# Three expert blocks issued at the release of their own places, in a hybrid mixer and mixture-of-experts layer

## The reference, cut to what matters

```python
logits = (t @ p['router_w'] + p['router_b']).astype(jnp.float32)
top_v, top_i = lax.top_k(logits, TOP_K)              # 4 of 32
for e in range(N_EXPERTS):                           # 32 experts, each 1024x2048 and 1024x1024
    gu = t @ p['moe_w_gu'][e] + p['moe_b_gu'][e]
    glu, lin = jnp.split(gu, 2, axis=-1)
    ...
    y = y + gates[:, e:e + 1] * (act @ p['moe_w_down'][e] + p['moe_b_down'][e])
```

## Time and profile before

| | us |
|---|---|
| median of 3 runs | 1330.65 |
| lowest, highest | 1329.86, 1331.6 |
| the profiled execution, its own time | 1328.54 |
| its span | 1326.6 |
| TensorE matmul busy | 1245.0 (94%) |
| VectorE, ScalarE busy | 400.6 (30%), 263.3 (20%) |

### The profile page before, as it was taken

The page is one execution under the profiler, slowest core; times in us unless marked ns, Lnnn a source line. Parts: engine busy times, 40 slices in busy tenths (PEclk is TensorE's granted clock), DMA queues, the critical chain, the costliest instruction groups (busy, mean ns, idle before and its releaser), DMA issues.

```text
span 1326.6 us, 21403 instructions
## 1 busy us (share of the span) xinstructions
PE 1245.0 (94%) x9094; PEld 588.9 (44%) x9094; DVE 400.6 (30%) x896; ACT 263.3 (20%) x595; POOL 54.2 (4%) x88
## 2 busy tenths in 40 slices
PE   5999999989999999999999999999989999999987
PEld 3456666678885333333333333333333333333333
DVE  1555756755443111122111121211122111122112
ACT  2333208553324110011010011100111010011001
POOL 0031200311200000000000000000000000000000
PEclk9999999999999999999999999999999999999999
DMA  9673420142369999999999999999999999999995
GB/s 385 259 293 147 163 100 0 67 128 69 105 249 373 423 428 426 428 426 427 430 427 427 429 428 427 430 428 427 429 427 427 428 427 427 427 428 428 426 427 237
DMA packets 38378, 453.97 MB, mean 342 GB/s; under 512 B 4288, under 2 KB 4544, under 8 KB 10016
## 3 DMA queue, kind: packets, MB, share of 16 engines
q1 hardware_dynamic: 38304, 452.86, 82.0%
HBM read 451.79 MB, written 1.05 MB: 341 GB/s over the span
## 4 chain that ended last, share of the span: by engine, by line
PE 82%; DMA 8%; DVE 6%; issue 2%; ACT 1%; SPq 0%; DVEq 0%
PE PS L1965 79%; DMA arena<-in_moe_w_gu 5%; DMA arena<-in_moe_b_down 2%; PE PS L2852 1%; DVE arena L1858 1%; DMA arena<-in_ada_first 1%; DVE arena L1861 1%; DVE arena L1864 1%; PE PS L2843 1%; DVE arena L1335 1%; DVE arena L1857 1%; PE PS L2447 0%; DVE arena L1958 0%; PE PS L1977 0%; ACT arena L984 0%
## 5 line engine op out<-in xcount | busy, mean ns | idle before, releaser
L1965 PE MATMUL PS<-arena 128*64 128x512 f32 (+11 forms) x8790 | 1209.2, 415 | 41.1 <-DMA arena<-in_ada_first 15.0
L1965 PEld LDWEIGHTS PS<-arena 64*64 64x64 f32 (+6 forms) x8790 | 559.2, 148 | 642.3 <-issue 576.4
L1857 DVE TENSOR_SCALAR arena<-PS 128x256 f32<-128x256 f32 x64 | 38.7, 604 | 510.5 <-PE PS L1965 510.5
L1167 ACT ACTIVATE arena<-arena 128x256 f32<-128x256 f32 x64 | 26.7, 417 | 482.0 <-DVE arena L1857 482.0
L1886 DVE TENSOR_TENSOR arena<-PS,arena 128x512 f32<-128x512 f32 x32 | 22.2, 692 | 212.8 <-PE PS L1965 212.8
L1177 ACT COPY arena<-PS 128x256 f32<-128x256 f32 x32 | 11.9, 373 | 279.3 <-PE PS L2843 279.3
L2852 PE MATMUL PS<-arena 128*128 128x128 f32 x128 | 26.3, 287 | 32.6 <-DVE arena L1864 32.6
L1158 ACT ACTIVATE arena<-PS,arena 128x128 f32<-128x128 f32 x128 | 48.2, 457 | 35.6 <-PE PS L1965 35.6
L1335 DVE SCALAR_TENSOR_TENSOR arena<-PS,arena 128x255 f32<-128x255 f32 (+5 forms) x68 | 32.6, 481 | 28.5 <-ACT arena L971 19.5
L2852 PEld LDWEIGHTS PS<-arena 128*128 128x128 f32 x128 | 14.2, 141 | 59.9 <-DVE arena L1864 43.0
L1623 DVE COPY arena<-PS 128x384 f32<-128x384 f32 (+2 forms) x48 | 23.5, 491 | 52.7 <-PE PS L1965 52.3
(11 more groups left out here) (264 smaller groups left out, 388.6 us busy)
## 6 DMA issues: line engine op xcount, KB each, us to landing
arena<-in_moe_w_gu SPq DMA_DIRECT2D x125, 2048.0 KB, 24.9
arena<-in_moe_w_down SPq DMA_DIRECT2D x63, 2048.0 KB, 26.3
arena<-in_ada_rest SPq DMA_DIRECT2D x16, 1024.0 KB, 4.7
arena<-in_w_in SPq DMA_DIRECT2D x5, 2048.0 KB, 8.5
arena<-in_ada_first SPq DMA_DIRECT2D x4, 2048.0 KB, 19.4
arena<-in_moe_w_gu SPq DMA_DIRECT2D x24, 256.0 KB, 2.9
arena<-in_tokens SPq DMA_DIRECT2D x1, 2048.0 KB, 8.3
arena<-in_w_out SPq DMA_DIRECT2D x2, 1024.0 KB, 5.8
```

Source lines behind the costliest of these rows:

```text
L1167: act.activation(sgm[:, 256 * half:256 * half + 256], glu[:, 256 * half:256 * half + 256], ACT.Sigmoid, scale=ALPHA).then_inc(sig_ready, 1)
L1857: dve.tensor_scalar(by_rest(glu), of_half(0), LIMIT, None, ALU.min).then_inc(glu_ready, 1)
L1965: ins = pe.matmul(out, lhsT, rhs, start=start, stop=stop, skip_group_check=skip)
```

## The change

SyncE no longer waits for ro before all four whole blocks. After the last small part of place 1 it waits until both directions of mt3 are emptied and loads place 3; waits until both directions of ol3 are emptied and loads the two held places; then waits for ro and loads place 7. The bias loads follow as before. All loads, their sizes and their targets stay the same; four waits are added on SyncE, and the order of the four blocks changes from 3, 7, held, held to 3, held, held, 7.

```diff
@@ -707,9 +707,15 @@
             for x in range(8):
                 at_round(40 + x)
                 load_block_part(1, x)
+            for d in range(2):
+                Q.emptied(sp, f"mt3{d}")
+            load_slot(3, 0, 3)
+            for d in range(2):
+                Q.emptied(sp, f"ol3{d}")
+            for x in range(2):
+                load_slot(RING + x, AHEAD * GROUP, 4 + x)
             Q.arrived(sp, "ro")
-            for r, e, s in ((3, 0, 3), (7, 1, 1), (RING, AHEAD * GROUP, 4), (RING + 1, AHEAD * GROUP, 5)):
-                load_slot(r, e, s)
+            load_slot(7, 1, 1)
             for x in range(2):
                 sp.dma_start(bgrow[32 * x:32 * x + E, :], a["moe_b_gu"][0, :, FF * x:FF * x + FF]).then_inc(late_in, 16)
             sp.dma_start(bdn[BD, 0:D], a["moe_b_down"][0]).then_inc(late_in, 16)
```

## The result

| | before | changed |
|---|---|---|
| median of 16 runs | 1330.64 us | 1334.93 us |
| lowest, highest | 1327.77, 1332.92 | 1332.31, 1338.39 |
| ratio, 95% interval | | 1.003, 1.0021 to 1.004 |
| profiled execution, span | 1328.54, 1326.6 | 1334.67, 1332.5 |

The change makes the kernel slower, by 4.3 us of median. The forecast was no change, 1330.2, with a range to 1332.4. The slow rival, which had ten chances in a hundred, is what happened.

A forecast was written before the change was run, and what follows sets the result against it. The prediction took a never-empty weight DMA stream, started at 413.74 by TensorE's progress, as the bound. Bias wait -0.74 plus fetch +0.3 gave -0.44 us: median 1330.65 becomes 1330.2, range 1328.6 to 1332.4.

The forecast's parts named there:

- slow rival: Instruction fetch at 374.4 waits behind a whole block, up to 4.9 us, then slow clock: +5.9, 1336.5; ten in a hundred.
- What bounds the kernel, and the worth of earlier bytes: Expert loop: never-empty weight stream sets the end, starting at 413.74 by TensorE's progress; rest of the 6.8 us worth 0.
- The waits on weight DMAs from 940 on: Sign of being right: TensorE's waits on weight DMAs from 940 on keep their sum of 14.7 us.
- The fast rival: Whole stream to the end moves with its first load: gain 6.8 us, time 1323.9; seven in a hundred.
- The loads move earlier, and nothing is queued behind the added waits: SyncE before ro: place 3 issued at about 372.2, held blocks at 376.2, 6.8 us earlier; added waits delay nothing.
- The bias wait: TensorE's wait for the last bias load, until 405.72, goes, so expert 0 starts earlier: -0.74 us.
- The fetch: TensorE's instruction fetch at 374.4, without slack, meets the load to place 3 and waits half a packet's turn: +0.3 us.
- The rule set against it: At the fetch: a DMA engine finishes a descriptor group before changing queues; sum about 4 us on the other side.
- The evidence I leaned on against the rival: Against the slow rival: packet length in the full stream, and no TensorE idle named issue between 378.96 and 412.

The follow-up runs named there:

- e6: Kernel before with only the three bias loads moved ahead of the four blocks behind ro; ratio 0.9991 to the kernel before.
- e2: Kernel before, but place 3 and the two held blocks are all issued when ol3 is emptied; ratio 1.0003 to the kernel before.
- e8: Changed kernel, but only half of place 3 (1024 KB) issued at mt3, the other half at ol3; ratio 1.0001 to the kernel before.
- e3: Changed kernel, but place 3 loaded in eight parts of 256 KB, all issued in a row at mt3; ratio 1.003 to the kernel before.
- e7: Changed kernel, but only one 256 KB part of place 3 issued at mt3, the other seven at ol3; ratio 0.9986 to the kernel before.
- e5: Kernel before with 50 small matmuls put first on TensorE, shifting fetch borders by 200 instructions; ratio 0.9967 to the kernel before.
- e12: Kernel before with 25 small matmuls put first on TensorE, shifting fetch borders by 100 instructions; ratio 0.9963 to the kernel before.
- e13: Kernel before with 64 small matmuls put first on TensorE, shifting fetch borders by a whole piece; ratio 1.0001 to the kernel before.
- e1: Changed kernel, but only place 3 issued early at mt3, the two held blocks behind ro again; ratio 1.002 to the kernel before.

## Why the prediction was wrong

*What bounds the kernel, and the worth of earlier bytes*: right, but for one sign. The waits on weight DMAs from 940 on, which were to keep their 14.7 us, came to 10.3; no run looks into why. The fast rival is out. In the changed kernel the weight queue carries next to nothing from 412 on until the reload of 417.81, and the 7 us by which the first block was earlier gave nothing.

*The loads move earlier, and nothing is queued behind the added waits*: right (371.89, 376.73).

*The bias wait*: right, -0.74 predicted; with what hangs on it -0.81 in the changed kernel, -0.82 in e6 and e2.

*The fetch*: the step that failed is "Full traffic does not stretch the packet, so what is left is the wait for its turn behind one packet of the load. ... Half of one on average: +0.3". I had the right fetch, its lack of slack, and the price list. The sum took the length of a packet, which is the one thing in those rows that says nothing of the wait ahead of it, as I wrote two paragraphs later, and priced the wait by a turn of 0.54 us. It was 2.5 to 3.0 us, five turns. In the profiled pair the standstill grew by 2.81 us, and with the clock behind it (+1.54) the term is 4.35 instead of 0.3. Less the bias wait that is 3.5 us, inside the 2.8 to 5.3 of the medians; the pair's remaining 0.52 was there ahead of the fetch.

*The rule set against it* told the right sign. The Trainium skill (DMA: Bandwidth & Descriptors, section on queues, rings and completion order) has an engine finish a group of descriptors of one queue before it turns to another. The fetch of the changed kernel went with most of the block through (1.85 of 2.1 MB, 356 GB/s from 372.8 to 378.0), and e8's at the end of its half: this agrees. e3 does not fit a group of one small DMA's size. The Trainium skill (Runtime: NRT & Kernel Launch, section on instruction fetch mechanics) says that code comes in blocks of 256 instructions and that the cost of a border is mostly hidden. The first half agrees with the packets of 0.02 MB and the pieces of 126 matmuls with 126 weight loads; the second holds for this kernel's long matmuls and not for its short ones, where nine stops from 262 to 380 us add up to 9.1 us in the kernel before.

*The evidence I leaned on against the rival*, no idle time named issue from 378.96 to 412 in a full stream, was worth nothing: the matmuls there are long (11 in 2 us, against 104 in 1.85 us ahead of the standstill), so a fetch may come 3 us late unseen. In e2 one was late there (381.8, 4.1 us behind the start of the 169; before it was at 378.2, 1.1 behind) and TensorE did not stop.

*The chances.* The rival had its mechanism, its place, a rule behind it and a row that could not speak against it. Ten in a hundred was too little, and the range should have reached its 1336.5.

## What to carry to other kernels

Before a load is moved forward over dense code, find the engine's instruction fetches in the trace (stops named issue, whole pieces of some 126 short matmuls) and ask what each will queue behind. What covered a late fetch here was long instructions ahead of the border (e2); what kept one from being late was a load that was over in time (e7) or issued later (e2). Price an unseen wait by what stands ahead in the queue, not by the length of the packet that waits. And take a pair of kernels with the same shift before you credit an edit with 0.3%: here 100 instructions without use at the start were worth more than the edit.

## What the runs showed that I had not expected

The place of the fetch borders alone moves this kernel by 0.33 to 0.37% (e5, e12), and not at all when they move by a whole piece (e13). Two nearly equal stops ahead of the same 16 matmuls left the clock in different levels: after 2.03 us at 987.4 in the kernel before it stayed at full speed and they took 3.68 us, after 2.17 us at 991.7 in the changed one it was at 0.50 and they took 5.38, 1.7 us more. e1 and e8 lost it there as well, after 2.29 and 2.15 us. Yet the way from the first reload to the output was no longer in these three than in the other variants. What decides about the clock is open.
